# Splits, a table load, averages and transfers moved in a two-block transformer kernel on one core

## What is computed

```python
# first block, for each of 2 layers
h = x @ w_in[l]                       # gives the inputs of four branches and the gates
proj = einsum('bsnc,ncd->bsnd', branches, w_o_branch[l])
merged = sum(sigmoid(merge + b_gate[l]) * proj, axis=2)
x = layer_norm(DEEPNORM_ALPHA * x + merged @ w_out[l], ln_g[l], ln_b[l])
# second block, for each of 2 layers
hx = rms_norm(x, g_mix[i]) * (1 + sc1) + sh1          # the same for ctx
zx = hx @ w_in[i]                                     # q, k, v, pool and fourier columns
mx = concatenate([latent_attention(q, k, v, kc, vc),
                  pool_mix(zx[..., KV_END:POOL_END], w_pool[i], pool_scale[i]),
                  fourier_mix(zx[..., POOL_END:], w_four[i])], axis=-1)
x = x + ga1 * (mx @ w_out[i])
x = x + ga2 * swiglu(rms_norm(x, g_ffn[i]) * (1 + sc2) + sh2, w_gate_up[i], w_down[i])
```

## Time and profile before

| | us |
|---|---|
| median of three runs | 3280.11 (3276.11 to 3282.70) |
| the profiled execution | 3281.99 |
| its span, first to last instruction | 3280.2 |
| TensorE busy (matmuls) | 3126.8, 95% |
| VectorE, GpSimd, ScalarE busy | 1514.1, 1480.8, 1167.7 |
| transfers | 86 GB/s in the mean |

### The profile page before, as it was taken

One profiled execution on the slowest core, in us unless ns is written; L12 is line 12 of the kernel. 1 busy time (PEld: TensorE's weight loads), 2 busy tenths in 40 slices (PEclk: granted clock), 3 DMA queues, 4 the chain that ended last, 5 costly groups with the idle time before them and its releaser, 6 DMA issues. The chain is left out here.

```text
span 3280.2 us, 51573 instructions
## 1 busy us (share of the span) xinstructions
PE 3126.8 (95%) x21064; PEld 2497.9 (76%) x21064; DVE 1514.1 (46%) x2359; ACT 1167.7 (36%) x1916; POOL 1480.8 (45%) x793
## 2 busy tenths in 40 slices
PE   8899999999898999999998998999999999899999
PEld 6785686887678756868876766888888876678887
DVE  7642284999666322949996365300100024520000
ACT  6325433422262344353223544322122234532221
POOL 4433553454344235535453366344234435645454
PEclk9999999999999999999999999999999999999999
DMA  3011132655220121325552200111121110022222
GB/s 135 9 35 64 52 109 71 212 199 192 88 65 3 41 71 49 112 91 198 202 183 91 89 14 27 58 63 60 58 71 65 61 66 33 20 84 97 96 97 97
DMA packets 76843, 281.28 MB, mean 86 GB/s; under 512 B 8640, under 2 KB 8640, under 8 KB 76096
## 3 DMA queue, kind: packets, MB, share of 16 engines
q1 hardware_dynamic: 76608, 277.98, 25.3%
HBM read 275.85 MB, written 2.10 MB: 85 GB/s over the span
## 5 line engine op out<-in xcount | busy, mean ns | idle before, releaser
L131 POOL TENSOR_TENSOR lows<-ring,highs 128x1024 fp32r<-128x1024 f32 x374 | 942.7, 2522 | 1494.5 <-ACT highs L123 1447.2
L155 PE MATMUL ps<-x_high,highs 128*128 128x512 f32 x2064 | 821.5, 398 | 42.3 <-ACT highs L123 24.2
L158 PE MATMUL ps<-x_low,highs 128*128 128x512 f32 x2064 | 807.8, 391 | 0.0
L123 ACT ACTIVATE highs<-ring 128x1024 fp32r<-128x1024 f32 x374 | 395.2, 1057 | 703.1 <-PE ps L155 344.8
L155 PEld LDWEIGHTS ps<-x_high,highs 128*128 128x128 f32 x2064 | 389.6, 189 | 146.9 <-issue 52.2
L158 PEld LDWEIGHTS ps<-x_low,highs 128*128 128x128 f32 x2064 | 389.7, 189 | 81.2 <-issue 3.6
L1817 DVE CUSTOM_DVE_ANT_0 BR<-BR 128x1024 f32<-128x1024 f32 x144 | 295.8, 2054 | 6.8
L2921 DVE TENSOR_TENSOR hidden_scratch<-ps,hidden_scratch 128x512 f32<-128x512 f32 x44 | 30.4, 692 | 546.1 <-PE ps L2167 537.6
L751 PE MATMUL ps<-x_high,lows 128*128 128x512 f32 x1024 | 252.9, 389 | 0.0
L751 PEld LDWEIGHTS ps<-x_high,lows 128*128 128x128 f32 x1024 | 192.2, 188 | 39.9
L2795 DVE SCALAR_TENSOR_TENSOR BR<-ps,mod,BR 128x512 f32<-128x512 f32 x72 | 47.4, 662 | 361.9 <-PE ps L167 361.9
(11 more groups left out here) (454 smaller groups left out, 5433.9 us busy)
## 6 DMA issues: line engine op xcount, KB each, us to landing
ring<-in_w SPq DMA_DIRECT2D x408, 512.0 KB, 3.5
BR<-in_ada SPq DMA_DIRECT2D x72, 512.0 KB, 3.6
merging<-in_ada SPq DMA_DIRECT2D x24, 512.0 KB, 3.5
X<-in_xT SPq DMA_DIRECT2D x4, 512.0 KB, 7.0
X<-in_memT SPq DMA_DIRECT2D x2, 1024.0 KB, 5.8
BR<-in_cond SPq DMA_DIRECT2D x4, 512.0 KB, 4.5
out<-BR SPq DMA_DIRECT2D x8, 256.0 KB, 4.5
cst<-in_cst SPq DMA_DIRECT2D x1, 1408.0 KB, 6.5
```

Of the source, the lines that this page charges most:

```text
L123: nc.scalar.activation(self.high(n), self.chunk(n), ACT.Copy).then_inc(self.hi_made, 1)
L131: nc.gpsimd.tensor_tensor(self.low(n), self.chunk(n), self.high(n).bitcast(F32), ALU.subtract).then_inc(self.lo_made, 1)
L155: mm = nc.tensor.matmul(ps, high, xhigh, start=start, stop=False)
L158: nc.tensor.matmul(ps, high, xlow, start=False, stop=False)
```

## The change

It moves work and removes none; one pooling goes to another engine.

1. Merge: TensorE runs k = 0 to 6 of both tiles, then k = 7 of both. ScalarE splits the second tile's chunk ahead of the last rounded row.
2. `output`: one chunk more is sent ahead of the clearing of semaphores, and in the second layer one more ahead of the context's rows. VectorE's `x_whole` stands one tile earlier.
3. `Norm.shifted`: in the second layer of the second block the split of the next chunk stands behind the third of the context's eight rows.
4. Second layer: the second pooling of x goes from GpSimd to VectorE, in the next block.
5. `Spectrum`: ScalarE's split of the output projection's second chunk moves ahead of the last copy of attention, GpSimd's into the next block.
6. `Project` with squares: the table load and ScalarE's last split move ahead of the last square, GpSimd's into the next block.

The diff, cut where it only closes what is shown:

```diff
@@ -476,8 +476,6 @@
...
                     finish(pairs[i - 2].group)
-            if spectrum is not None:
-                spectrum.closing_scalar(act)
...
@@ -497,8 +495,6 @@
...
                     ahead.pool(pool, i)
-            if spectrum is not None:
-                spectrum.closing_pool(pool)
...
@@ -1743,10 +1739,10 @@
...
                             mm.then_inc(S("product"), 1)
-                for t in range(2):
+                for t, ks in ((0, range(DK - 1)), (1, range(DK - 1)), (0, (DK - 1,)), (1, (DK - 1,))):
                     pe.wait_ge(S("gate"), 29 + t)
                     stream.wait_high(pe, n0 + 48 + t)
-                    for k in range(DK):
+                    for k in ks:
                         pe.wait_ge(S("merged_low"), k + 1)
...
@@ -1776,9 +1772,9 @@
...
                         nc.scalar.activation(CB, CB, ACT.Silu).then_inc(S("silu_c"), 1)
+                stream.hi(nc, act, n0 + 48 + 2)
                 act.wait_ge(S("merged"), 24)
                 nc.scalar.activation(MH[:, 7, :], MG, ACT.Copy).then_inc(S("merged_high"), 1)
-                stream.hi(nc, act, n0 + 48 + 2)
...
@@ -1839,10 +1835,10 @@
...
         def _(sp):
-            stream.send(sp, n0 + RING)
+            stream.send(sp, n0 + RING + 1)
             clear(sp, other)
             if context is not None:
-                context.sync(sp, S)
+                context.sync(sp, S, n0)
             stream.send(sp, n0 + 8 + RING - 1)
...
@@ -1893,8 +1889,11 @@
...
             v = nc.vector
+            def whole(t):
+                v.tensor_tensor(RR[:, t, :], XH[:, t, :].bitcast(F32), XL[:, t, :].bitcast(F32), ALU.add).then_inc(S("x_whole"), 1)
+
+            whole(0)
             for t in range(8):
-                v.tensor_tensor(RR[:, t, :], XH[:, t, :].bitcast(F32), XL[:, t, :].bitcast(F32), ALU.add).then_inc(S("x_whole"), 1)
                 dve.wait_ge(S("product"), t + 1)
...
@@ -1903,6 +1902,8 @@
...
                     v.tensor_tensor(RUN, RR[:, 0, :] if t == 1 else RUN, RR[:, t, :], ALU.add).then_inc(S("run"), 1)
+                if t < 7:
+                    whole(t + 1)
                 if context is not None:
...
@@ -1996,9 +1997,10 @@
...
-        def sync(self, sp, S):
+        def sync(self, sp, S, n):
             sp.dma_start(par[:, :], A["par2"][0]).then_inc(S("par"), 16)
             sp.dma_start(cst[:, 0:early], A["cst2"][:, 0:early]).then_inc(S("cst"), 16)
+            stream.send(sp, n + RING + 2)
             sp.dma_start(cT.rearrange("p k t -> p (k t)"), A["ctxT"]).then_inc(S("c_in"), 16)
...
@@ -2184,11 +2186,13 @@
...
-            def shifted(self, act, s):
+            def shifted(self, act, s, upto=None):
                 nm = s["name"]
...
                     nc.scalar.activation(s["h"][:, t, :], self.slots[nm][:, t % 4, :], ACT.Identity, bias=mod[:, self.shift + t, s["k"]:s["k"] + 1]).then_inc(self.S("h" + nm), 1)
+                    if t == 2 and upto is not None:
+                        stream.hi(nc, act, upto)
...
@@ -2198,7 +2202,7 @@
...
                 for i, s in enumerate(self.sts):
-                    self.shifted(act, s)
+                    self.shifted(act, s, upto + 2 if i and then else None)
                     if i == between:
...
@@ -2517,6 +2521,8 @@
...
                     stream.lo(nc, pool, n0 + 9 + c)
+                    if c and not update:
+                        continue
                     if c == 0 and layer == 0:
...
@@ -2583,8 +2589,10 @@
...
             def _(dve):
-                if update:
-                    done, arrays = [0], [mixed[:, i * XB:(i + 1) * XB] for i in range(3)]
+                done, arrays = [0], [mixed[:, i * XB:(i + 1) * XB] for i in range(3)]
+                if not update:
+                    pooling(dve, nc.vector, S("dve_step"), done, PL[1], T, 1, counts_of["x"], arrays)
+                else:
                     for c in range(2):
...
@@ -2657,6 +2665,8 @@
...
                     nc.scalar.activation(MX[:, (6 if i < 4 else 4) + c, :], PS[:, 7, :], ACT.Copy, scale=1.0 if i < 4 else par_col("pool_scale", c)).then_inc(S("spectrum_out"), 1)
+                elif i == len(pairs) + 1:
+                    stream.hi(nc, act, at["out"] + PARTS)
...
@@ -2666,12 +2676,6 @@
...
                 stream.lo(nc, pool, at["out"] + 1)
-
-            def closing_scalar(self, act):
-                stream.hi(nc, act, at["out"] + PARTS)
-
-            def closing_pool(self, pool):
-                stream.lo(nc, pool, at["out"] + PARTS)
...
@@ -2758,6 +2762,9 @@
...
                     if squares is not None:
+                        if m == 7:
+                            nc.scalar.activation(spare[:, 0:1], C("ones"), ACT.Ln).then_inc(S("table"), 1)
+                            stream.hi(nc, act, self.first + self.kt + 2)
                         for s in full:
...
@@ -2765,9 +2772,6 @@
...
                 stream.hi(nc, act, self.first + self.kt + 1)
-                if squares is not None:
-                    stream.hi(nc, act, self.first + self.kt + 2)
-                    nc.scalar.activation(spare[:, 0:1], C("ones"), ACT.Ln).then_inc(S("table"), 1)
...
@@ -2780,7 +2784,7 @@
...
                             nc.gpsimd.tensor_tensor(stats[nm], stats[nm], squares[nm][:, m % 2, :], ALU.add).then_inc(S("summed" + nm), 1)
-                stream.lo(nc, pool, self.first + self.kt + (1 if squares is None else 2))
+                stream.lo(nc, pool, self.first + self.kt + 1)
...
```

## The result

The changed kernel takes 3253.67 us (median of four runs, 3252.12 to 3258.40), 0.9924 of the kernel before, with a 95% interval of 0.9911 to 0.9936. The forecast was 3253. Its profiled execution took 3252.12 us with a span of 3250.3: 29.9 us less than the one of before.

A forecast was written before the change was run, and what follows sets the result against it. TensorE, busy almost throughout, bounds the kernel; 5.9 + 2.5 + 5.7 + 4.2 + 6.5 + 3.7 = 28.5 us, less 1.0 for clock, 27.5 off 3281.99 gives 3254.5, 3252.6 as median, rounded to 3253; range 3243 to 3263.

The forecast's parts named there:

- Two output tiles: End of the merge, both layers: second tile's matmuls cover the wait for the last merged row; 5.9 us gained.
- The 1.6 us of clock in the second layer: Merge's end, second layer: stretch 1.6 us longer than the first layer's, at clock 0.86 against 1.00; claimed to go too.
- Constants' transfers: Second layer's output block: chunk's 3.54 us pause goes, 2.5 us of wait returns at the fifth tile; 2.5 kept.
- the clock's 1.6 us: Second layer's output block: low clock behind the chunk's pause goes, 1.6 us of the 5.1 counted before 2.5 came off.
- Splits at the end of attention: Output projection's start, twice: TensorE starts 1.8 us sooner despite GpSimd's split holding up VectorE, plus clock; 5.7 us.
- Ends of projections: Three block ends with sums of squares: pauses shrink, 0.3 barrier and 0.4 later sums kept at each; 4.2 us gained.
- Averages: Second layer, before the transforms: 4.7 us pause shrinks to 1, slow clock goes, VectorE's averages barely hidden; 6.5 us.
- The split inside the norm: Second layer's norm: 2.01 us wait for ScalarE's split and 1.7 of low clock go; 3.7 us gained.
- Whole rows: VectorE's whole rows change places with work that had slack on both sides; nothing gained.
- The 1.0 us for the clock's moments: Taken off the sum: shifted later work may lose the clock behind pauses of 1.5 to 2 us; 1.0 us.
- B: Pauses handed on, first the context chain costing all the chunk gave; 15.5 us gained, 3265; chance 0.18.
- A: Pauses stay away: VectorE passes GpSimd's split, context lands early, clock holds; 36 us gained, 3244; chance 0.17.

The follow-up runs named there:

- u_tiles: Changed kernel with the merge's last two tiles' matmuls in the old order, ScalarE's third split kept where the change puts it; 3259.17 us.
- u_const: Changed kernel with the whole order of transfers undone, both chunks sent as before (behind the constants, behind the context); 3259.04 us.
- u_ctx: Changed kernel with only the context's transfer put ahead of the fifth tile's chunk again; 3250.05 us.
- e_early: Changed kernel with both splits of the output projection's second chunk made inside attention, ScalarE's one pair earlier; 3245.61 us.
- u_ends: Changed kernel with the ends of the output and down projections as before (table load, ScalarE's and GpSimd's splits moved back); 3261.85 us.
- u_pool: Changed kernel with the second layer's second average on GpSimd again, in the projection block; 3260.97 us.
- u_norm: Changed kernel with ScalarE's split inside the second layer's norm behind all eight context rows again; 3258.63 us.
- the two added edits: Changed kernel with the output projection's second split inside attention, and the fifth tile's split ahead of the context's squares and sums; alone 3245.61 and 3250.89, together 3246.30 us.
- e_fill: Changed kernel with 12 unread filler matmuls between attention's last product and the output projection's first; 3250.38 us.
- again: Changed kernel measured once more with nothing edited; 3253.30 us, ratio 0.9921 to the kernel before.

## Why the prediction came out right, step by step

The median was 0.7 us from the forecast, which is closer than the steps deserve. Five of them were right in mechanism and about right in size. The rest is luck: by the table the places give 26.2 us where the parts added up to 28.5, the constants' part was too high by some 2, and the 1.0 taken off for the clock, which had no such loss behind it, made up for half of that.

- **Two output tiles**, 5.9 forecast: 6.6 between the profiles, of which u_tiles confirms 2.5 in each layer. The 1.6 us of clock in the second layer were taken from one stretch as if they belonged to the pause. u_tiles had the pause without them. What failed here is only that term of the sum.
- **Constants' transfers**, 2.5 forecast: 0.2 to 0.6. The chain was right: the context landed 13.3 us behind the block's start (forecast 13), and TensorE waited 2.52 us at the fifth tile for GpSimd's split (forecast 2.5). The step that failed is the clock's 1.6 us, which I kept as gained. The new wait drops the clock as the old one did, in six of eight profiles. And the pause to be removed, 3.54 us in the earlier trace rows, was 3.15 in u_const. The chunk ahead of the context, which the prediction counted as a delay of the context alone, cost more than it gave (u_ctx).
- **Splits at the end of attention**, 5.7 forecast: 5.0 (2.2 and 2.8). Pauses of 3.76 and 3.98 against 3.9, VectorE's subtraction ended 0.55 us behind the split as in the earlier trace rows (2.25 us long and not about 3, since it began 0.65 behind the split), and a clock that still fell. No run undoes this part; the 5.0 are between profiles. e_early shows what the hold-up cost: 1.45 and 1.56 us of pause, and in one of the two places the clock as well.
- **Ends of projections**, 4.2 forecast: 3.9. The pauses shrank to 0.30 as forecast, and the sums came later as forecast. The time is kept because the norm's chain begins at the barrier; TensorE's pause alone would mislead, as u_ends shows.
- **Averages**, 6.5 forecast: 6.4, with 6.0 coming back in u_pool. The steps on VectorE took 5.3 us (estimate 5.4), and the split's chain ended within 0.03 us of them.
- **The split inside the norm**, 3.7 forecast: 2.9 and 4.1 by the two profiles, and 3.9 back in u_norm.
- **Whole rows**, nothing forecast: 0.7 to 1.0 us. "Slack on both sides" was true of seven tiles. At the eighth VectorE is the block's last engine, and TensorE's pause of 1.82 us at the block's end, which the prediction doesn't look at, was the sign.
- **The 1.0 us for the clock's moments**: no such loss is to be seen. The clock's part is a spread of several us between executions: the same code arrives between 1724.7 and 1733.1 at one point.

Of the rivals, B's first link held nearly whole (the context's chain cost almost all that the chunk gave) and its others didn't; A's way of getting more, VectorE not held up and the context's chain out of the way, didn't happen by itself but is what the two added edits did.

## What to carry to other kernels

Ask of every split, table load or transfer that you move not only whether the pause goes, but which instruction is behind it in its new queue, and do it before the long chain rather than behind it: the fifth tile's split cost 2.5 us of pause behind 5.4 us of sums and nothing ahead of them. Where VectorE starts a block, keep GpSimd's two-input work out of its first microseconds. Measure a part of a few microseconds by a distance between two marks around it in several profiles, and take a lower clock behind a pause as a chance of a cost, not as a cost.

## What the runs showed of the hardware

- A VectorE subtraction with both inputs in SBUF does not proceed beside GpSimd's split: 2.25 to 2.31 us in 22 places where it began inside one, 0.69 in the six where it didn't.
- Whether TensorE's granted clock falls behind a pause is not a matter of that pause alone. Around a pause of 2.15 us it read 0.86 (before), with 2.17 at the same place 1.00 (u_tiles), behind 3.15 us 1.00 (u_const), behind 0.73 us 0.61 (e_fill).
- Matmuls that only fill time are not free where the clock is low: twelve took 4.58 us in place of 3.00, and came out behind the row they were to wait for (e_fill).
- Where two chunks are issued together at the start of the second layer's output block, the first one's split begins 4.6 to 4.8 us behind the block's first product in three profiles (changed, again, u_tiles) and 3.3 to 3.7 in nine others; where the chunk goes alone (u_const) it is 3.5. What delays it in some executions is open.
